# Four LayerNorms in a two-layer trunk: 12 of 16 feature blocks centred early about a provisional mean, the first activation chunk in halves, MLPs opened with two panels in turn

## What is computed

```python
h = x * (1.0 + scale) + shift                     # scale, shift, gate: projections of silu(c)
y = mixer(h)            # or: jnp.square(jax.nn.relu(h @ w_up)) @ w_down
x = layer_norm(ALPHA * x + (1.0 + gate) * y, w, b)

def layer_norm(x, w, b):
    mu = mean(x);  xc = x - mu;  var = mean(xc * xc)
    return xc * rsqrt(var + 1e-5) * w + b
```

## Time and profile before

| | |
|---|---|
| median of three runs | 3200.02 us |
| the profiled execution's own time | 3199.55 us |
| its span, first to last instruction | 3197.8 us |
| TensorE busy | 3064.6 us, 96% of the span |
| VectorE, ScalarE, GpSimd busy | 54%, 41%, 10% |
| mean granted TensorE clock | 0.98 of 2.4 GHz |
| chain of waits: TensorE, DMA, VectorE, ScalarE | 88%, 4%, 4%, 2% |

### The profile page before, as it was taken

How to read it: one execution, slowest core, us unless ns; L and a number is a source line. 1 busy time by engine, 2 the same in 40 slices (tenths; PEclk the granted TensorE clock), 3 DMA queues, 4 the chain that set the end, 5 groups by cost and what they waited for, 6 DMA issues and landing times.

```text
span 3197.8 us, 66605 instructions
## 1 busy us (share of the span) xinstructions
PE 3064.6 (96%) x26916; PEld 2858.7 (89%) x26916; DVE 1721.5 (54%) x2402; ACT 1302.2 (41%) x1690; POOL 304.1 (10%) x306
## 2 busy tenths in 40 slices
PE   6899999998999999999999899999989999999997
PEld 3689898878799999999998888987979999999997
DVE  2477776664544444444445666665464454454444
ACT  1355555542433333333333544444354343343433
POOL 0012221111300000000001301110130000000001
PEclk8999999999999999999999999999989999999998
DMA  9988777887777677676776665575435555555551
GB/s 351 322 292 260 245 253 250 263 279 255 243 244 245 201 241 231 216 246 210 236 245 220 209 230 161 191 231 180 150 118 166 165 165 165 166 166 166 168 167 64
DMA packets 541634, 685.59 MB, mean 214 GB/s; under 512 B 22226, under 2 KB 469258, under 8 KB 541066
## 3 DMA queue, kind: packets, MB, share of 16 engines
q1 hardware_dynamic: 484402, 625.43, 60.1%
q10 hardware_dynamic: 56960, 56.21, 5.4%
HBM read 650.88 MB, written 30.67 MB: 213 GB/s over the span
## 4 chain that ended last, share of the span: by engine, by line
PE 88%; DMA 4%; DVE 4%; ACT 2%; issue 2%; POOL 0%; ACTq 0%; SPq 0%; DVEq 0%; POOLq 0%
PE main L523 26%; PE main L525 25%; PE main L524 25%; PE bank L533 4%; DMA raw<-in_w_ada 2%; DMA gl_s<-in_state_gla 1%; PE bank L657 1%; DVE z L2160 1%; ACT ln_h L1205 0%; DMA raw<-in_hg_w_out 0%; PE bank L1076 0%; DVE hg_s L1981 0%; ACT w_hi L1194 0%; PE bank L551 0%; DVE a_lo L1731 0%
## 5 line engine op out<-in xcount | busy, mean ns | idle before, releaser
L1726 DVE TENSOR_TENSOR w_lo<-raw,w_hi 128x1024 fp32r<-128x1024 f32 x804 | 991.9, 1235 | 1239.0 <-ACT w_hi L1194 1235.0
L1194 ACT ACTIVATE w_hi<-raw 128x1024 fp32r<-128x1024 f32 x804 | 850.3, 1059 | 1574.3 <-PE main L525 1485.6
L523 PE MATMUL main<-a_hi,w_hi 128*128 128x288 f32 x4272 | 1298.7, 304 | 27.1 <-DVE a_lo L1731 21.2
L525 PE MATMUL main<-a_hi,w_lo 128*128 128x288 f32 x4272 | 1267.9, 297 | 0.0
L524 PE MATMUL main<-a_lo,w_hi 128*128 128x288 f32 x4272 | 1267.0, 297 | 0.0
L523 PEld LDWEIGHTS main<-a_hi,w_hi 128*128 128x128 f32 x4272 | 811.2, 190 | 66.3 <-issue 41.9
L524 PEld LDWEIGHTS main<-a_lo,w_hi 128*128 128x128 f32 x4272 | 810.5, 190 | 4.3 <-issue 1.7
L525 PEld LDWEIGHTS main<-a_hi,w_lo 128*128 128x128 f32 x4272 | 810.4, 190 | 0.0
L523 PE MATMUL main<-act_hi,w_hi 128*128 128x288 f32 x2048 | 605.9, 296 | 0.0
L525 PE MATMUL main<-act_hi,w_lo 128*128 128x288 f32 x2048 | 604.9, 295 | 0.0
L524 PE MATMUL main<-act_lo,w_hi 128*128 128x288 f32 x2048 | 601.9, 294 | 0.0
(11 more groups left out here) (295 smaller groups left out, 1951.8 us busy)
## 6 DMA issues: line engine op xcount, KB each, us to landing
raw<-in_w_ada SPq DMA_DIRECT2D x384, 512.0 KB, 6.4
raw<-in_w_up SPq DMA_DIRECT2D x256, 512.0 KB, 3.8
raw<-in_w_down SPq DMA_DIRECT2D x256, 512.0 KB, 3.5
raw<-in_hg_w_in SPq DMA_DIRECT2D x128, 512.0 KB, 6.5
raw<-in_gla_w_in SPq DMA_DIRECT2D x100, 512.0 KB, 3.8
raw<-in_hg_w_out SPq DMA_DIRECT2D x32, 512.0 KB, 4.9
gl_s<-in_state_gla ACTq DMA_DIRECT2D x32, 512.0 KB, 6.3
out_new_gla_sample<-gl_s ACTq DMA_DIRECT2D x32, 512.0 KB, 4.8
```

Of the source, the lines that this page charges most:

```text
L523: mm(out, hi, x_hi[:, kb, :], start=kb == 0, stop=False)
L525: last = mm(out, lo, x_hi[:, kb, :], start=False, stop=kb == KB - 1)
L1194: F(w_hi[:, st.split_slot(g)].rearrange("p k n -> p (k n)"), raw[:, slot, :], ACT.Copy).then_inc(hi_ready, 1)
L1726: V.tensor_tensor(w_lo[:, s].rearrange("p k n -> p (k n)"), raw[:, slot, :], w_hi[:, s].rearrange("p k n -> p (k n)").bitcast(F32), ALU.su ...
```

## The change

- **Provisional mean.** GpSimd adds up only the first 12 blocks (`EARLY`). In tile 26 of the last 32 before each LayerNorm, between its matmuls, TensorE sums that over the partitions. VectorE centres blocks 0 to 13 about this mean in steps 27, 29, 30 and 31, and ScalarE squares them in steps 28, 30 and 31. The terms c1, c0 and awb of the next h are computed in step 26.
- **Last panel.** Its tile 31 is run with its two output blocks one after the other (`apart`); each block has its own residual, centring and addition to a sum `ds` of blocks 12 to 15 (`residual_block`).
- **After the last panel.** The true mean differs from the provisional one by the sum of `ds` over the features divided by 2048, since the first 12 blocks sum to zero about the provisional mean. VectorE takes this remainder as `mu`, the variance is the mean square less `mu` squared, and the remainder is subtracted (`shift`) before the scaling.
- **Pieces.** The chunks are now blocks 0-1, 2-3, 4-7, 8-11, 12-15, and the first tile starts on blocks 0-1. The casts and splits of tiles 3 to 6 are put between the pieces.
- **Opening.** An MLP's first eight tiles take panels 0 and 1 in turn, so each chunk feeds two tiles. The order of the DMAs is changed to match. The conditioning tiles of the first two LayerNorms move: 8 come behind the variance sum, the other 8 between the first tiles of the next stage.
- The MLP's first and last turns are written out on ScalarE and VectorE.

```diff
+PAIRED = [(0, 0), (1, 0), (0, 1), (1, 1), (0, 2), (1, 2), (0, 3), (1, 3)]
+MLP_OPENING = (first_weights(0, 3) + lead_tiles(0, 0, 8) + first_weights(3, 4) + lead_tiles(0, 8, 12) + first_weights(4, 5) +
+               lead_tiles(0, 12) + first_weights(5, 6))
+for step in range(3, 64):
+    MLP_OPENING += [("a", i) for i in range(32) if step == max(6 * (i // 4), 3)] + first_weights(step + 3, min(step + 4, 64))
-LOW = Stage(MLP0, 1, 4, {0: KB}, emptied_by="A")
+LOW = Stage(MLP0, 1, 4, {0: 8, 1: 2, 2: 3, 3: 3}, emptied_by="A")
+PIECES = [(0, 2), (2, 4), (4, 8), (8, 12), (12, 16)]
+EARLY = 12
...
# TensorE
-        def layer_norm(i, event, filler=None):
-            if filler:
-                filler(0, 5)
+        def provisional_mean(i):
             pe.wait_ge(ln_sum, i + 1)
             mm(b4[:, 0:T], ones[:, :], mu[:, :], start=True, stop=True).then_inc(ln_mean, 1)
+        def layer_norm(i, filler=None):
+            for c in range(4):
+                pe.wait_ge(ln_squared, 6 * i + (c + 1 if c < 3 else 5))
...
+            last.then_inc(ln_parts, 1)
+            pe.wait_ge(ln_dsum, i + 1)
+            mm(b7[:, 0:T], ones[:, :], mlp_b["ds"][:, :], start=True, stop=True).then_inc(ln_delta, 1)
+            pe.wait_ge(ln_squared, 6 * i + 6)
+            mm(b4[:, 0:T], ones[:, :], mlp_b["sq"][:, KB - 1, :], start=True, stop=False)
+            pe.wait_ge(ln_parts_out, i + 1)
+            mm(b4[:, 0:T], ones[:, :], rstd[:, :], start=False, stop=True).then_inc(ln_var, 1)
             if filler:
-                filler(RING, KB)
+                filler(0, RING)
...
# TensorE
+                    p, t = PAIRED[s] if n == 0 and s < 8 else divmod(s, 4)
+                    if n == 0 and s == 0:
+                        between = first_chunk(event)
+                    elif n == 0 and s in (2, 4, 6):
+                        pe.wait_ge(a_ready, a_at(event, t))
+                    elif n == st.iters - 1 and s == 58:
+                        between = lambda: provisional_mean(1 if st is MLP0 else 3)
+                    if with_ada and n == 0 and s in (1, 2):
+                        ln0_ada(4 * s + 4, 4 * s + 8)
...
# ScalarE
+        def layer_norm(i, e, casts=None):
+            square(i, 4, 14, 15)
+            square(i, 5, 15, 16)
...
+            for n in range(3):
+                h_piece(i, e, n)
+            cast(casts, 0, 3)
+            h_piece(i, e, 3)
+            cast(casts, 0, 4)
+            h_piece(i, e, 4)
+            cast(casts, 0, 5)
+            cast(casts, 0, 6)
...
+        filler_copy(LOW.a0 + KB, ADA_LOW, ln["ada"][:, :])
+        panel_done(LOW, 0, 3)
+        F(gl["low"][:, :], main[:, LOW.bank(0) + 1, 0:T], ACT.Copy).then_inc(panel_read["A"], 1)
         act.wait_ge(G["gk2_set"], 1)
         for b in range(4):
             gl_load(0, b)
-        for s in range(4):
-            cast(LOW, 0, s + AHEAD)
-        panel_done(LOW, 0, 3)
-        F(gl["low"][:, :], main[:, LOW.bank(0) + 1, 0:T], ACT.Copy).then_inc(panel_read["A"], 1)
...
# VectorE
+        def residual_block(st, n, p, layer, gate, i, norm):
+            src, kb = panel(st, p), KB - 2 + i
+            at = gate * KB + kb
+            V.scalar_tensor_tensor(out=z[:, kb, 0:TP], in0=src[:, i, 0:TP], scalar=mod[:, layer, at, 0:1],
+                                   in1=z[:, kb, 0:TP], op0=ALU.mult, op1=ALU.add)
+            last = V.tensor_tensor(seqs(zs[:, i:i + 1, :]), seqs(src[:, i:i + 1, TP:T]),
+                                   per_token(mod[:, layer, at:at + 1, 1:NSEQ]), ALU.mult)
...
+            step(V.tensor_tensor(z[:, kb, TP:T], z[:, kb, TP:T], zs[:, i, :], ALU.add))
+            V.tensor_tensor(z[:, kb, :], z[:, kb, :], mu[:, :], ALU.subtract).then_inc(ln_centered, 1)
+            dve.wait_ge(ln_centered, 6 * norm + 5 + i)
+            last = V.tensor_tensor(mlp_b["ds"][:, :], mlp_b["ds"][:, :], z[:, kb, :], ALU.add)
...
+        def early_norm(i, e, s):
+            if s == 26 and e is not None:
...
+            elif s == 27:
+                dve.wait_ge(ln_mean, i + 1)
+                step(V.tensor_scalar(mu[:, :], b4[:, 0:T], 1.0 / (EARLY * P), None, ALU.mult))
+                center(0, 0, 4)
+            elif s == 29:
+                center(1, 4, 8)
+            elif s == 30:
+                center(2, 8, 12)
+            elif s == 31:
+                center(3, 12, 14)
+                dve.wait_ge(ln_squared, 6 * i + 1)
+                dve.wait_ge(ln_centered, 6 * i + 4)
+                step(V.tensor_tensor(mlp_b["ds"][:, :], z[:, 12, :], z[:, 13, :], ALU.add))
...
+            dve.wait_ge(ln_delta, i + 1)
+            step(V.tensor_scalar(mu[:, :], b7[:, 0:T], 1.0 / D, None, ALU.mult))
+            ds = mlp_b["ds"][:, :]
+            step(V.tensor_tensor(ds, mu[:, :], mu[:, :], ALU.mult))
+            dve.wait_ge(ln_var, i + 1)
+            V.scalar_tensor_tensor(out=rstd[:, :], in0=b4[:, 0:T], scalar=1.0 / D, in1=ds, op0=ALU.mult, op1=ALU.subtract
+                                   ).then_inc(ln_spread, 1)
+            shift(0, 4)
             dve.wait_ge(ln_rstd, i + 1)
...
+            def piece(n):
+                first, last = PIECES[n]
+                if n >= 2:
+                    shift(first, last)
+                scale(first, last)
+                if n >= 3:
+                    dve.wait_ge(a_ready, A_BASE[e] + n - 1)
+                dve.wait_ge(ln_scaled, 5 * i + n + 1)
+                sample_h(first, last)
...
+            piece(0)
+            piece(1)
+            low(0)
+            piece(2)
+            low(1)
+            low(2)
+            split(splits, 0, 3)
+            piece(3)
+            low(3)
+            split(splits, 0, 4)
+            piece(4)
+            low(4)
+            split(splits, 0, 5)
+            split(splits, 0, 6)
```

More of the change, by code:

```diff
@@ L1153, in _ @@
         for s in range(4):
[L1154 to L1155 removed]
+            if s:
+                first = LOW.first_ada(s)
+                ln1_ada(first, first + LOW.ada[s])
+                pe.wait_ge(a_ready, a_at(3, s))
+            gemm(LOW, 0, s, 0, s, a_hi, a_lo, blocks=(1,), between=None if s else first_chunk(3))
+        ada_turn(ADA_LOW, [b7[:, 0:P], b7[:, P:2 * P]], ln["ada"])
         def gl_iteration(n, prev):
@@ L1556, in mlp @@
+            for s in range(4 if opening else 0, 64):
+                if not (last_n and st is MLP1 and s + AHEAD >= 64):
                     cast(st, n, s + AHEAD)
-                if s % 4 == 0 and 4 <= s <= 32:
+                if with_ada and opening and s == 4:
+                    filler_copy(MLP0.a0 + KB, ADA_LN0, mlp_b["ada"][:, 0:256])
+                if s % 4 == 0 and (8 if opening else 4) <= s <= 32 or opening and s == 7:
                     p = s // 4 - 1
@@ L2183, in mlp @@
+            piece(0)
[12 more added lines that the diff above has]
+            split(splits, 0, 6)
         def mlp(st, e, n, layer, with_ada, last_n=False):
-            for s in range(64):
-                if not (last_n and s + AHEAD >= 64):
+            opening = isinstance(n, int) and n == 0
@@ L2186, in mlp @@
+            for s in range(4 if opening else 0, 64):
+                if not (last_n and st is MLP1 and s + AHEAD >= 64):
                     split(st, n, s + AHEAD)
-                if s % 4 == 0 and 4 <= s <= 32:
+                if with_ada and opening and s == 6:
+                    mod_update(1, 16, 1, ADA_LN0, [b7])
+                if s % 4 == 0 and (8 if opening else 4) <= s <= 32 or opening and s == 7:
                     p = s // 4 - 1
@@ L2333, in _ @@
         V.memset(gl["atts"][:, :], 0.0).then_inc(G["att_set"], 1)
-        for s in range(4):
-            split(LOW, 0, s + AHEAD)
         gl_iteration(0, False)
```

344 lines of the change are left out of this document (189 added, 155 removed).

## The result

The changed kernel takes 3206.4 us (median of 14 runs, 3201.7 to 3212.8) against 3198.6 of the kernel before on the same chip (14 runs, 3194.3 to 3203.8): ratio 1.0024, 95% interval 1.0016 to 1.0032. It is 7.8 us slower; 1.2 us faster was forecast. The time lies in the range, the sign is the wrong one. A second comparison gave 1.0034 (1.0021 to 1.0048).

A forecast was written before the change was run, and what follows sets the result against it. TensorE, busy 96%, bounds the kernel, so only its waits pay. Terms +1.6 - 2.7 - 0.6 + 4.9 - 2.0 = 1.2 us won: 3198.35 profiled, median 3198.8; range 3189 to 3207.

The forecast's parts named there:

- Head: Start of the first three LayerNorms: first product at T+11.3 (T: end of the last product before), 9.2 us earlier.
- Pieces: Later pieces on VectorE, 8.7 us each, one after the other: low 4 at T+36.7, split 5 at T+37.9.
- Third LayerNorm: Before MLP1: TensorE waits 5.6 us before tile 5, plus 1.6 us for lower clock; 0.6 us lost.
- Second: Second LayerNorm (LOW, then GLA): 1.7 us lost at LOW's last half tile, 1 us waiting for gl_gk; 2.7 lost.
- First: First LayerNorm (MLP0): the conditioning batch behind tile 6 starts at T+44.7 instead of T+46.3; 1.6 us won.
- No clock is lost: First LayerNorm: the wait before tile 5 is short, with 12 conditioning tiles between tiles 1 and 4.
- the DMAs hold out: First LayerNorm: at 1.63 us a tile, the 15th conditioning tile lands at T+32.5; tile 4 can end before split 5.
- the weights come late: Rival: 2.1 us per tile instead of 1.63 delays the first two LayerNorms; 6.7 us, 3205.5; chance 0.14.
- Last: Last LayerNorm with the output: copies end at T+23.7 instead of T+28.7, 0.6 us charged for lowered clock; 4.9 us won.
- Moved means: Four provisional means moved into TensorE's stream, 0.49 us each; 2.0 us lost.
- The ports: Rival: GpSimd gets in first at the shared ports, 6.7 us in each of three LayerNorms; 3219; chance 0.07.

The follow-up runs named there:

- half the bytes: The changed kernel with its 16 conditioning tiles at the first LayerNorm loaded only half; T0 to T1 906.9 us, not the 903.5 to 904.5 expected.

## Why the prediction was wrong, step by step

- **Head.** First product at T+11.2 in the third LayerNorm (T+11.3 forecast), pause until T+15.8 (15.9). Right. In the first it came at T+12.5, in other profiles at T+11.2 to T+12.8.
- **Pieces.** Low 4 at T+36.9 (36.7), split 5 at T+38.3 (37.9). Right, and the run with VectorE's order changed shows that they were the cause.
- **Third LayerNorm**, -0.6 forecast: the right wait, 5.59 us (5.6), but the lowered clock was charged 1.6 us, by half a tile, and lasted for a whole one: 2.8, and 1.4 in another profile. In the changed kernel's profile the loss to tile 5's end is 2.5 us, not 0.6. The wait was right, the term of the clock too small.
- **Second**, -2.7 forecast: the step whose size failed. To the gate matmul 5.2 us were lost against the first profile of before (3.6 against the second): 2.0 for the half tile's later start (1.7 in all forecast), its lowered clock until 1787 instead of 1784, and 1.5 for gl_gk (1.0). I had sized the load's landing at 4.9 us though it was to stand behind four state loads; in ten profiles it took 5.6 to 12.5, and TensorE waited 0.9 to 6.8. What a wait costs behind itself was left out, 1.4 to 2.9 us where the clock fell. T1 to T2 lost 5.8 in two profiles and 8.1 as the mean of six, against 3.2 forecast.
- **First**, +1.6 forecast: the step whose sign failed. "No clock is lost" and "the DMAs hold out" were both wrong. The granted clock was 0.52 from T+18 to T+21. I worked with the rate of the ring and not with its order: a load stands in SP's queue behind splits that are themselves late, and the first conditioning tiles had moved from T to T+7.1, so around the head the queues stood still. Windows from T-0.6 to T+12.4, of the changed kernel and of the kernel before:

```profile
837.00:850.00 13.00, 9.84 (x105) 4.79 (x103) 10.21 (x24) 5.39 (x11) 1.37 (x2) 0.87 0.36 113
...
841.10:854.10 13.00, 8.03 (x104) 3.35 (x103) 9.04 (x14) 5.06 (x5) 1.65 (x2) 1.00 0.88 304
```

  So 113 GB/s against 304. In this profile the batch starts 0.7 us later than before and tile 8 2.1 us later, where 1.6 were to be won; as a mean of four profiles T0 to T1 lost 3.7. Part of that is the late first product. In the one of the four in which it came at T+11.2 the batch starts at T+45.2 (44.7 forecast), and T0 to T1 is 905.5, +1.7; the other three read 907.1 to 909.2. In that one the weights come late behind it, which the forecast left out:

```profile
888.47 0.64 PE L555 MATMUL bank<-raw,c_t 128*32 128x256 f32 x8 [0.62 <-DMA raw<-in_w_ada]
893.06 0.40 PE L543 MATMUL main<-a_hi,w_hi 128*128 128x288 f32 x1 [0.57 <-ACT mlp_r L1642]
```

  The rival "the weights come late" was right in the place and wrong in the reason, since half the bytes changed nothing.
- **Last**, +4.9 (28.7 less 23.7 is 5.0): measured 5.7. The clock stayed at 1.00 up to T+9 there, past the matmuls that the chain waits for, so the 0.6 charged for it fell away.
- **Moved means**, 2.0: 0.4 each where it could be read.
- **The ports.** Weighed rightly: 1.6 us in the chain up to tile 5, not 6.7. The exclusive lock of the Trainium skill (SBUF — State Buffer, section "SBUF: two separate sides") lets whichever engine starts second wait for the other's whole instruction. The rows show GpSimd as the one that gives way: its affine got long, 6.55 us for four, while VectorE's operations lost 0.05 and 0.30 us each, not a whole affine.

By the means over all unedited profiles the misses are 4.8 us in the first, 4.9 in the second and 2.1 in the third LayerNorm, less 0.8 in the last. So two steps failed: the first LayerNorm's gain, which rested on a full clock and on loads in time, and the second's price for a wait and for the load behind four others. The three misses have the same sign, and in all three something was left out that follows a wait of TensorE: a lowered clock, or loads that the wait itself had held back. They are not all of it: the late first product and the 1.8 us in GLA come on top.

What stays open: why the clock fell already at T+4 in some executions and not in others (below), why it stayed low for 3 or for 6 us behind the same wait, and what made GLA longer behind its second gate matmul. That the last LayerNorm's change alone on the kernel before gives 5.7 us was not tried.

## What to carry to other kernels

When an engine serves both a chain and the hand-over of weights, write out its queue with the hand-overs in it: the chain was 9 us shorter at its head, and the third LayerNorm won nothing from it until the next piece stood ahead of the low part that waits for ScalarE. Price a new wait of the bounding engine with what follows it (1.4 to 2.8 us of lowered clock behind 5.6 us here; a load behind four others took up to 12.5 us instead of 4.9), and look at what stands behind it in every queue, not only at rates.
